# Attention probabilities normalized on VectorE, directly behind the inverse sums

## What is computed

```python
def sliding_window_attention(q, k, v, sinks):
    ...
    def block(j):                      # 128 queries, 256 keys
        s = jnp.einsum('bqkgd,bskd->bkgqs', qj, kj) * scale
        valid = band & (ki + j * A_WINDOW - A_WINDOW >= 0)
        s = jnp.where(valid, s, -jnp.inf)
        sink = jnp.broadcast_to(sink_logits, s.shape[:-1] + (1,))
        p = jax.nn.softmax(jnp.concatenate([s, sink], axis=-1), axis=-1)[..., :-1]
        return jnp.einsum('bkgqs,bskd->bqkgd', p, vj)
    out = lax.map(block, jnp.arange(n_blocks))
    return jnp.moveaxis(out, 0, 1).reshape(bsz, seq, A_Q)

def swa_layer(hn, positions, w_in, q_g, k_g, sinks, w_out):
    ...
    a = sliding_window_attention(q, k, v, sinks)
    return (a * jax.nn.silu(z)) @ w_out.astype(F32)
```

## Time and profile before

| what | value |
|---|---|
| kernel, median of 3 runs | 3034.83 us (3031.55 to 3037.38) |
| the profiled execution | 3025.52 us, span 3023.7 us |
| mean granted TensorE clock | 0.957 of full |
| PE busy in the span | 2765.6 us (91%) |
| DVE busy | 1558.9 us (52%) |
| ACT busy | 1103.1 us (36%) |
| POOL busy | 640.8 us (21%) |

### The profile page before, as it was taken

How to read it: one execution, slowest core, us unless ns; L and a number is a source line. 1 busy time by engine, 2 the same in 40 slices (tenths; PEclk the granted TensorE clock), 3 DMA queues, 4 the chain that set the end, 5 groups by cost and what they waited for, 6 DMA issues and landing times. The chain is left out here.

```text
span 3023.7 us, 36865 instructions
## 1 busy us (share of the span) xinstructions
PE 2765.6 (91%) x13163; PEld 2195.2 (73%) x13163; DVE 1558.9 (52%) x3227; ACT 1103.1 (36%) x2442; POOL 640.8 (21%) x526
## 2 busy tenths in 40 slices
PE   4799998999999799689997699997899999899999
PEld 2677887888888678578785577776677777667776
DVE  5565771556655456453223666664534431456664
ACT  2611221222222222334331455553522222366664
POOL 0004661544545100032232000000100000033332
PEclk7899999999999899899998899999899999999999
DMA  7216446454454465698896465662422324512221
GB/s 252 95 67 149 146 145 155 138 149 144 147 157 138 151 218 178 211 251 238 256 276 193 133 178 168 165 171 79 167 73 74 88 76 122 166 60 89 85 85 63
DMA packets 454027, 445.66 MB, mean 147 GB/s; under 512 B 157556, under 2 KB 349388, under 8 KB 450380
## 3 DMA queue, kind: packets, MB, share of 16 engines
q1 hardware_dynamic: 350340, 337.75, 38.0%
q10 hardware_dynamic: 103504, 105.54, 10.8%
HBM read 282.06 MB, written 162.74 MB: 147 GB/s over the span
## 5 line engine op out<-in xcount | busy, mean ns | idle before, releaser
L2771 PE MATMUL a_pg<-a_hT,a_whl 128*128 128x512 f32 x640 | 256.7, 401 | 3.4 <-DVE a_whl L878 3.4
L2772 PE MATMUL a_pg<-a_hT,a_whl 128*128 128x512 f32 x640 | 251.1, 392 | 0.0
L2773 PE MATMUL a_pg<-a_hT,a_whl 128*128 128x512 f32 x640 | 250.9, 392 | 0.0
L884 PE MATMUL p_g<-hT,w_hl 128*128 128x512 f32 x512 | 212.2, 415 | 0.0
L830 PE MATMUL pg<-hT,w_hl 128*128 128x512 f32 x512 | 206.3, 403 | 6.5 <-DVE w_hl L878 6.5
L832 PE MATMUL pg<-hT,w_hl 128*128 128x512 f32 x512 | 201.9, 394 | 0.0
L831 PE MATMUL pg<-hT,w_hl 128*128 128x512 f32 x512 | 201.7, 394 | 0.0
L886 PE MATMUL p_g<-hT,w_hl 128*128 128x512 f32 x512 | 200.2, 391 | 0.0
L885 PE MATMUL p_g<-hT,w_hl 128*128 128x512 f32 x512 | 199.8, 390 | 0.0
L2771 PEld LDWEIGHTS a_pg<-a_hT,a_whl 128*128 128x128 f32 x640 | 121.4, 190 | 42.0 <-DVE a_whl L878 11.4
L2773 PEld LDWEIGHTS a_pg<-a_hT,a_whl 128*128 128x128 f32 x640 | 121.3, 189 | 26.3
(11 more groups left out here) (502 smaller groups left out, 6848.9 us busy)
## 6 DMA issues: line engine op xcount, KB each, us to landing
s_wt<-s5w_d SPq DMA_DIRECT2D x64, 354.0 KB
vo_d<-e_stage ACTq DMA_DIRECT2D x64, 256.5 KB, 8.5
w_raw<-in_ev_w_in SPq DMA_DIRECT2D x32, 512.0 KB, 5.7
s5w_d<-gate_sums SPq DMA_DIRECT2D x32, 512.0 KB, 3.0
shared<-h_d SPq DMA_DIRECT2D x28, 512.0 KB, 4.1
arena<-in_ada_w SPq DMA_DIRECT2D x8, 1536.0 KB, 11.6
e_ada_w<-in_ada_w SPq DMA_DIRECT2D x32, 384.0 KB, 7.4
a_raw<-in_od_w_in SPq DMA_DIRECT2D x40, 256.0 KB, 3.4
```

Of the source, the lines that this page charges most:

```text
L884: nc.tensor.matmul(out, w(0, k), x(0, k), start=(k == 0), stop=False)
L2771: mm(bank, w[:, 0, k, :], x[:, 0, k, :], start=(k == 0), stop=False)
L2772: mm(bank, w[:, 0, k, :], x[:, 1, k, :], start=False, stop=False)
L2773: last = mm(bank, w[:, 1, k, :], x[:, 0, k, :], start=False, stop=(k == KC - 1))
```

## The change

The block of GpSimd in `attend` goes, and with it the semaphore `inv_ready`. The multiply of the probabilities by the inverse sums is now the third instruction of `inverse(G)` on VectorE, with the same operands; VectorE waits for its own reciprocal ahead of it (`L`), and the multiply signals `p_ready`, for which `turn(G)` waits as before. The orders of TensorE, ScalarE and SyncE are unchanged.

```diff
@@ attend: the semaphores
-        s_done, s_read, max_ready, exp_ready, inv_ready, p_ready, p_turned, pT_ready = S(
-            "s_done s_read max_ready exp_ready inv_ready p_ready p_turned pT_ready")
+        s_done, s_read, max_ready, exp_ready, p_ready, p_turned, pT_ready = S(
+            "s_done s_read max_ready exp_ready p_ready p_turned pT_ready")
@@ attend: GpSimd
-            @block.gpsimd
-            def _(pool):
-                def divide(G):
-                    pool.wait_ge(inv_ready, G + 1)
-                    p = sc[G % 3]
-                    nc.gpsimd.tensor_tensor(p, p, st[G % 3][:, 4].unsqueeze(2).broadcast_to([P, 4, 2 * P]), ALU.mult).then_inc(p_ready, 1)
-
-                for G in range(STEPS):
-                    divide(G)
@@ attend: VectorE, inverse(G)
                     v.wait_ge(exp_ready, G + 1)
                     L(tt(s[:, 4], s[:, 3], s[:, 2], ALU.add))
-                    nc.vector.reciprocal(s[:, 4], s[:, 4]).then_inc(inv_ready, 1)
+                    L(nc.vector.reciprocal(s[:, 4], s[:, 4]))
+                    p = sc[G % 3]
+                    tt(p, p, s[:, 4].unsqueeze(2).broadcast_to([P, 4, 2 * P]), ALU.mult).then_inc(p_ready, 1)
```

## The result

The changed kernel takes 3087.62 us (median of 4 runs, 3077.53 to 3092.51) against 3036.11 us of the kernel before (4 runs, 3031.55 to 3037.7). The ratio is 1.0172, with a 95% interval of 1.015 to 1.0194: it is slower by 1.7%. The profiled execution took 3077.53 us with a span of 3075.7 us, 52.0 us more than the span before.

A forecast was written before the change was run, and what follows sets the result against it. TensorE bounds attention at 5.853 us a step; with the multiply a ScalarE-VectorE loop of 6.64 us takes over. 2.4 + 51.4 - 2.1 = 51.7 us more makes about 3087 us, range 3072 to 3107 us.

The forecast's parts named there:

- The price of the multiply: VectorE, attention: the added 128x1024 multiply takes 1.22 us, 1.13 us to the next start; bounded by 0.68 and 1.90 us.
- The wait for the reciprocal: VectorE, attention: waiting for its own reciprocal adds 0.03 us, at most 0.08; the multiply starts 0.21 us behind the reciprocal.
- The second loop: Attention: exponentials, cast, y's low part, sum, reciprocal, maxima across ScalarE and VectorE; 5.416 us beside TensorE's 5.853, growing to 6.64.
- this ring: Attention: the ScalarE-VectorE round of waits without TensorE, from one step's exponentials to the next; 6.64 us with the multiply inside.
- Opening: Attention steps 1 and 2, no cast before them yet: one multiply ahead of each, 2 x 1.22 = 2.4 us more.
- The 61 rounds: Attention steps 3 to 63: 61 x 6.64 = 405.0 us against 353.6 us before, 51.4 us more.
- The end: Last transposes: TensorE's backlog is gone, start 4.6 us behind the last exponentials' start instead of 6.75, giving back 2.1 us.
- Hidden: Attention: VectorE's idle time takes the multiply, TensorE stays the bound, 3035 to 3041 us; 6 in 100.
- The clock: TensorE, attention: gaps make the chip grant it less clock, at a mean of 0.79 giving 3127 us; 6 in 100.
- The other prices: VectorE's multiply takes 0.68 us, giving 3053 us, or GpSimd's 1.90 us, giving 3130 us; 3 in 100 each.
- Faster: TensorE's 0.33 us pause before the transposes is a wait for GpSimd's signal and goes: 21 us, 3014 us; 1 in 100.
- a shorter way round: Attention: VectorE's other instructions become shorter without GpSimd beside them; named as what would most easily make the forecast wrong.

## Why the prediction was right

*The price of the multiply.* Taken as 1.22 us from the 128x1024 rows of another stage; measured 1.224 us, and 1.15 us from its start to the next (1.13 taken). Spreading the inverse sums over 256 columns did not make it longer. The wait for the reciprocal was 0.21 us from start to start, as taken. Neither bound, 0.68 nor 1.90 us, was needed.

*Which loop.* The second loop of 5.416 us was read from the opening steps, where TensorE did not yet cover it. That is the step which carries the forecast: with the 1.22 us added it gave 6.64 us, and the trace has 6.643. The experiments show that it is this ring: the same multiply outside it costs nothing that can be told from noise, other work of the same size inside it costs nearly the same, twice the work costs 1.26 us more in a round, and another link taken out gives back most.

*The sum.* Opening 2.4 us: step 2's exponentials start at 2643.11 against 2640.50, 2.6 us. The 61 rounds: 405.2 us against 353.6, 51.6 us where 51.4 stood. The end gives back 2.2 us where 2.1 stood; TensorE's last products but one do wait for ScalarE's copies, but the transposes are not held beyond VectorE's 4.5 us. The spans differ by 52.0 us against 51.7 forecast. On the median, the agreement to under 1 us (3087.62 against 3087) is partly luck: the kernel before alone spans 6 us over its 4 runs here, and 16 us over the 23 runs on another chip.

*The rivals.* Hidden: the result itself shows it wrong. Its arithmetic was sound, as the multiply behind the maxima shows: VectorE does have the time. Its mistake is to take idle time for slack. By the Trainium skill (Perfetto Trace Analysis, Identifying the Most-Contended Engine) one looks for the busiest engine. The trace of the kernel before agrees: TensorE was busy for 100% of the stretch, and by its weight loads, one of the two figures by which the section judges TensorE, for 71%, still more than VectorE's 60%. For the kernel after it does not: no engine's occupancy (TensorE 89%, its weight loads 63%, VectorE 70%, ScalarE 51%, GpSimd 0%) names the bound. The clock: 1.00 at 89% busy. The other prices: the multiply took 1.22 us, so neither holds. Faster: the pause on which it rested is no wait for GpSimd, for it is 0.33 us in the changed kernel and with no multiply at all (16.9 us, 51 times), and moving the wait did not change it. The reason given for the range, a shorter way round once GpSimd is quiet, did not show either: the custom instruction of the maxima takes 0.54 us in both kernels.

## What to carry to other kernels

Before moving work to an engine that looks idle, follow its list around: from the instruction behind the new one, who waits for it, what stands behind that on the other engine, and whether the path comes back. Its round time is easiest to read where the main engine is not yet loaded, in the first steps of a pipeline; slack is the difference of the two rounds (here 0.44 us), not the idle share (here 40%). And work in such a ring may often be put one place further on in the same list, behind what others wait for, at next to no cost: here the ratio was 1.0003, and 1.0013 at the upper end of its interval.

## What was not expected of the hardware

GpSimd and VectorE, each with a 128x512 float32 multiply of operands in SBUF at the same time, were not equal: VectorE's took 0.69 us, GpSimd's 1.54 to 1.55 us in all 64 steps where 1.06 us is the median of the nearest row, although it started only 0.04 to 0.05 us later. The Trainium skill (SBUF — State Buffer, Who interferes with whom) says that a VectorE instruction with two inputs in SBUF and a GpSimd instruction that reads SBUF contend for shared ports, that these are an exclusive lock, and that the order of issue decides which of the two is blocked. The direction agrees. The loss is 0.49 us against that row and 0.60 us against half of the whole multiply, and VectorE's was still running for 0.64 us, so how complete the block is can't be told. The nearest row has a trace of the same thing: of its 64 instructions 15 took 1.10 us or longer, and all 15 overlapped a 128x512 instruction of VectorE in SBUF (L1126 or L1101), but so did 7 that took 1.06 us. There the loss could fall on VectorE too: its L1101, 0.69 us as a median of 64, took 1.04 and 1.05 us in the two places where an instruction of GpSimd had started 0.5 to 0.6 us ahead of it.

A granted clock of 0.92 in the kernel with the doubled multiply left the time of its steps at the loop's 7.90 us, where nobody waited long for TensorE. In the opening of the kernel with the multiply behind the maxima VectorE did wait for the scores at a granted clock of 0.50, and that round was 1.48 us longer than before.
